# x and the first weight unit loaded, split and multiplied in halves at the start of a decoder trunk kernel

## The reference

```python
def rms_norm(x, g):
    y = xf * lax.rsqrt(jnp.mean(xf * xf, axis=-1, keepdims=True) + EPS)
    return (y * g.astype(jnp.float32)).astype(x.dtype)

def swiglu(h, w_gate, w_up, w_down):
    return (jax.nn.silu(h @ w_gate) * (h @ w_up)) @ w_down

def reference(x, meta, ...):
    h = jnp.concatenate([jnp.broadcast_to(meta...), x], axis=1)
    for l in range(DEPTH):
        f = swiglu(rms_norm(h, ffn1_pre[l]), ffn1_wg[l], ffn1_wu[l], ffn1_wd[l])
        h = h + FFN_RESID * rms_norm(f, ffn1_post[l])
        ...  # mixer (pool, short convolution, gated linear attention), then the second FFN in the same form
    return h[:, N_META:]
```

## Time and profile before

| | us |
|---|---|
| median of 3 runs (1104.22 to 1105.97) | 1104.71 |
| span of the profiled execution, first to last instruction (no other time of it is given) | 1104.4 |
| PE busy in it | 1066.6 |
| DVE, ACT, POOL busy | 659.6, 505.7, 290.9 |
| first product of x and weights (L1134) starts at | 16.20 |
| first product of the loop behind units 0 and 1 (L1102) starts at | 32.06 |

### The profile page before, as it was taken

One profiled execution on the slowest core, in us unless ns is written; L12 is line 12 of the kernel. 1 busy time (PEld: TensorE's weight loads), 2 busy tenths in 40 slices (PEclk: granted clock), 3 DMA queues, 4 the chain that ended last, 5 costly groups with the idle time before them and its releaser, 6 DMA issues.

```text
span 1104.4 us, 20089 instructions
## 1 busy us (share of the span) xinstructions
PE 1066.6 (97%) x8288; PEld 1029.7 (93%) x8288; DVE 659.6 (60%) x607; ACT 505.7 (46%) x543; POOL 290.9 (26%) x194
## 2 busy tenths in 40 slices
PE   8999999999899999999989999999998989999997
PEld 7999999988798999999979999998987989999996
DVE  5745454498776844454486444536997676555543
ACT  6444444455445543443454434435543555434441
POOL 2333330036300433340024333200372023324100
PEclk8999999999999999999999999999999999999998
DMA  9765445634324455436636553456533327563531
GB/s 297 215 197 158 143 134 182 211 129 138 115 78 153 150 166 181 155 106 196 216 101 217 176 179 120 157 174 202 156 111 116 102 91 222 166 203 113 181 106 39
DMA packets 167646, 172.55 MB, mean 156 GB/s; under 512 B 6652, under 2 KB 160536, under 8 KB 167592
## 3 DMA queue, kind: packets, MB, share of 16 engines
q1 hardware_dynamic: 167416, 171.70, 49.0%
q10 hardware_dynamic: 176, 0.07, 0.0%
HBM read 170.70 MB, written 1.05 MB: 156 GB/s over the span
## 4 chain that ended last, share of the span: by engine, by line
PE 83%; DVE 12%; ACT 2%; issue 1%; POOL 1%; DMA 1%; SPq 0%; ACTq 0%; POOLq 0%; DVEq 0%
PE ps L1102 23%; PE ps L1103 23%; PE ps L1104 23%; PE ps L1134 3%; PE ps L1119 3%; PE ps L1135 3%; DVE h L682 2%; DVE w_lo L640 2%; DVE x_lo L668 2%; PE ps L1296 2%; DVE f L674 1%; PE ps L1363 1%; ACT w_hi L424 1%; DVE r_post L985 1%; PE ps L1168 1%
## 5 line engine op out<-in xcount | busy, mean ns | idle before, releaser
L640 DVE TENSOR_TENSOR w_lo<-raw,w_hi 128x2048 fp32r<-128x2048 f32 (+2 forms) x182 | 396.0, 2180 | 321.6 <-ACT w_hi L424 321.2
L1102 PE MATMUL ps<-x_hi,w_hi 128*128 128x272 f32 (+1 forms) x1616 | 464.6, 288 | 1.6 <-DVE w_lo L640 1.6
L1103 PE MATMUL ps<-x_lo,w_hi 128*128 128x272 f32 (+1 forms) x1616 | 465.2, 288 | 0.0
L1104 PE MATMUL ps<-x_hi,w_lo 128*128 128x272 f32 (+1 forms) x1616 | 464.3, 287 | 0.0
L424 ACT ACTIVATE w_hi<-raw 128x2048 fp32r<-128x2048 f32 (+2 forms) x182 | 321.2, 1769 | 229.5 <-PE ps L1104 183.6
L1102 PEld LDWEIGHTS ps<-x_hi,w_hi 128*128 128x128 f32 x1616 | 305.9, 189 | 4.1 <-DVE w_lo L640 2.2
L1103 PEld LDWEIGHTS ps<-x_lo,w_hi 128*128 128x128 f32 x1616 | 305.4, 189 | 0.1
L1104 PEld LDWEIGHTS ps<-x_hi,w_lo 128*128 128x128 f32 x1616 | 305.2, 189 | 0.0
L1102 PE MATMUL ps<-hid_hi,w_hi 128*128 128x272 f32 (+1 forms) x528 | 152.6, 289 | 0.0
L1104 PE MATMUL ps<-hid_hi,w_lo 128*128 128x272 f32 (+1 forms) x528 | 151.3, 287 | 0.0
L1103 PE MATMUL ps<-hid_lo,w_hi 128*128 128x272 f32 (+1 forms) x528 | 150.5, 285 | 0.0
(11 more groups left out here) (163 smaller groups left out, 1047.8 us busy)
## 6 DMA issues: line engine op xcount, KB each, us to landing
raw<-in_ffn_wg SPq DMA_DIRECT2D x88, 512.0 KB, 4.0
raw<-in_ffn_wu SPq DMA_DIRECT2D x88, 512.0 KB, 4.9
raw<-in_ffn_wd SPq DMA_DIRECT2D x96, 384.0 KB, 3.2
raw<-in_w_in SPq DMA_DIRECT2D x40, 512.0 KB, 4.7
raw<-in_ffn_wd SPq DMA_DIRECT2D x32, 256.0 KB, 3.2
raw<-in_w_out SPq DMA_DIRECT2D x16, 512.0 KB, 4.5
x_tok<-in_x SPq DMA_DIRECT2D x2, 512.0 KB, 6.7
raw<-in_w_in SPq DMA_DIRECT2D x4, 256.0 KB, 3.5
```

Of the source, the lines that this page charges most:

```text
L640: v_.tensor_tensor(w_lo[:, slot, 0:n], raw[:, slot, 0:n], f32(w_hi[:, slot, 0:n]), ALU.subtract)\
L1102: pe.matmul(out_, wh, xh, start=first, stop=False)
L1103: pe.matmul(out_, wh, xl, start=False, stop=False)
L1104: return pe.matmul(out_, wl, xh, start=False, stop=last)
```

## The change

x comes in four DMAs of half the columns each (channel tiles 0 to 3, then 4 to 7), two on SP's queue and two on ACT's. Unit 0 comes in four DMAs too: k = 0 and 1 of both matrices, then k = 2 and 3. SP's order is meta, x, unit 0's first half, x, unit 0's second half, unit 1, and the parameters and constants behind it. PE transposes tiles 0 to 3, runs the `w_hi x_hi` and `w_lo x_hi` products of k = 0 and 1, transposes tiles 4 to 7, and only then does the `x_lo` products and the second half of unit 0. ACT and DVE split unit 0 in two halves, in between the tiles of x.

```diff
@@ SP
-            def first_loads():
-                sp.dma_start(meta_tok[:, :], meta).then_inc(x_in, 16)
-                for tt in range(2):
-                    sp.dma_start(x_tok[:, tt], x[0, tt * P:(tt + 1) * P, :]).then_inc(x_in, 16)
-                for name, src, per in rows[1:]:
-                    load_rows(sp, name, src, per, par_in)
+            def first_unit():
+                wg, wu, _ = weights(phases[0])
+                dst = raw[:, 0].rearrange("p (s k n) -> p s k n", s=2, k=4)
+                sp.dma_start(meta_tok[:, :], meta).then_inc(x_in[0], 16)
+                for half in range(2):
+                    cols, ks = slice(half * 512, half * 512 + 512), slice(2 * half, 2 * half + 2)
+                    landed = raw_in[0] if half else first_in
+                    sp.dma_start(x_tok[:, 0, cols], x[0, 0:P, cols]).then_inc(x_in[half], 16)
+                    sp.dma_start(dst[:, 0, ks], wg[:, ks, 0:256]).then_inc(landed, 16)
+                    sp.dma_start(dst[:, 1, ks], wu[:, ks, 0:256]).then_inc(landed, 16)
             def constant_loads():
+                for name, src, per in rows[1:]:
+                    load_rows(sp, name, src, per, par_in)
@@ ACT
+            for half in range(2):
+                cols = slice(half * 512, half * 512 + 512)
+                act.dma_start(x_tok[:, 1, cols], x[0, P:2 * P, cols]).then_inc(x_in[half], 16)
...
-            high_unit(0, UNIT)
             act.wait_ge(par_ready, 1)
-            for kk in range(KT):
+            for kk in range(2):
+                high_x(kk)
+            first_high(0)
+            for kk in range(2, 4):
+                high_x(kk)
+            first_high(1)
+            for kk in range(4, KT):
                 high_x(kk)
             high_unit(1, UNIT)
@@ DVE
-            low_unit(0, UNIT)
...
-            for kk in range(KT):
+            def copy_h(kk):
                 v_.wait_ge(ends_tr, kk + 2)
                 v_.tensor_copy(h[:, kk, :], ps[:, kk, 0:T]).then_inc(h_ready, 1)
-            for kk in range(KT - 1):
-                low_x(kk)
+            for kk in range(4):
+                copy_h(kk)
+            first_low(0)
+            low_x(0)
+            low_x(1)
+            first_low(1)
+            for kk in range(4, KT):
+                copy_h(kk)
+                low_x(kk - 2)
             low_unit(1, UNIT)
+            low_x(KT - 2)
             low_x(KT - 1)
@@ PE
+            pe.wait_ge(x_in[0], 48)
+            for kk in range(4):
+                transpose_x(kk)
+            def first_unit():
+                view = up_view(0)
+                pe.wait_ge(h_ready, 4)
+                for half in range(2):
+                    if half:
+                        pe.wait_ge(unit_lo, 1 + RING)
+                    else:
+                        pe.wait_ge(first_lo, 1)
+                    for kk in range(2 * half, 2 * half + 2):
+                        pe.wait_ge(xh_ready, kk + 1)
+                        for mm in range(4):
+                            pe.matmul(ps[:, mm, 0:T], view(w_hi, kk, mm), x_hi[:, kk, :], start=kk == 0, stop=False)
+                            pe.matmul(ps[:, mm, 0:T], view(w_lo, kk, mm), x_hi[:, kk, :], start=False, stop=False)
+                    if half == 0:
+                        pe.wait_ge(x_in[1], 32)
+                        for kk in range(4, KT):
+                            transpose_x(kk)
+                    for kk in range(2 * half, 2 * half + 2):
+                        pe.wait_ge(xl_ready, kk + 1)
+                        for mm in range(4):
+                            last = pe.matmul(ps[:, mm, 0:T], view(w_hi, kk, mm), x_lo[:, kk, :], start=False,
+                                             stop=False)
+                last.then_inc(unit_used, 1)
```

More of the change, by code:

```diff
@@ L227, in trunk @@
         mix_in = sem("mix_in")
-        x_in = sem("x_in")
+        x_in = [sem(f"x_in{i}") for i in range(2)]
+        first_in = sem("first_in")
+        first_hi = sem("first_hi")
+        first_lo = sem("first_lo")
         zeroed = sem("zeroed")
@@ L365, in _ @@
                     for j in range(2):
-                        up_unit(j, u0 + j + 1, slice(0, 256))
                         if j == 0 and u0 == 0:
-                            first_loads()
+                            first_unit()
+                        else:
+                            up_unit(j, u0 + j + 1, slice(0, 256))
                         if j == 1 and u0 == 0:
@@ L456, in high_x, with first_high @@
                 act.activation(x_hi[:, kk, :], h[:, kk, :], ACT.Copy, scale=col("ffn1_pre", 0, kk)).then_inc(xh_ready, 1)
-            high_unit(0, UNIT)
-            act.wait_ge(par_ready, 1)
-            for kk in range(KT):
+            def first_high(half):
+                tiles = lambda w: w[:, 0].rearrange("p (s k n) -> p s k n", s=2, k=4)[:, :, 2 * half:2 * half + 2]
+                if half:
+                    act.wait_ge(raw_in[0], 32)
+                else:
+                    act.wait_ge(first_in, 32)
+                act.activation(tiles(w_hi), tiles(raw), ACT.Copy).then_inc(unit_hi if half else first_hi, 1)
+            act.wait_ge(par_ready, 1)
+            for kk in range(2):
[5 more added lines that the diff above has]
+            for kk in range(4, KT):
                 high_x(kk)
@@ L713, in _, with first_low @@
             v_.sem_inc(up_evac, 1)
-            low_unit(0, UNIT)
+            def first_low(half):
+                tiles = lambda w: w[:, 0].rearrange("p (s n) -> p s n", s=2)[:, :, 512 * half:512 * half + 512]
+                if half:
+                    v_.wait_ge(unit_hi, 1)
+                else:
+                    v_.wait_ge(first_hi, 1)
+                v_.tensor_tensor(tiles(w_lo), tiles(raw), f32(tiles(w_hi)), ALU.subtract)\
+                  .then_inc(unit_lo if half else first_lo, 1)
             v_.wait_ge(ends_tr, 1)
@@ L1186, in _, with transpose_x @@
               .then_inc(ends_tr, 1)
-            pe.wait_ge(x_in, 48)
-            for kk in range(KT):
+            def transpose_x(kk):
                 if kk == KT - 1:
@@ L1195, in _ @@
                 last.then_inc(ends_tr, 1)
-            pe.wait_ge(h_ready, 4)
+            pe.wait_ge(x_in[0], 48)
[5 more added lines that the diff above has]
+                for half in range(2):
+                    if half:
+                        pe.wait_ge(unit_lo, 1 + RING)
+                    else:
+                        pe.wait_ge(first_lo, 1)
[14 more added lines that the diff above has]
+                last.then_inc(unit_used, 1)
             for ph in phases:
@@ L1208, in group @@
                             u = u0 + ja + j
+                            if u == 0 and not j and waits:
+                                first_unit()
+                                continue
                             unit(u % RING, i4 + (u + 1 + RING), up_view(u % RING), range(4 * j, 4 * j + 4), range(4),
```

2 lines of the change are left out of this document (1 added, 1 removed).

## The result

| | before | after |
|---|---|---|
| median, us | 1105.28 (4 runs, 1104.22 to 1105.97) | 1112.91 (4 runs, 1112.14 to 1113.71) |
| span of the profiled execution | 1104.4 | 1110.2 (its own time 1112.14) |
| start of unit 1's high part on ACT (H) | 17.50 | 21.29 |
| first product of the loop behind units 0 and 1 | 32.06 | 36.71 |
| from there to the end | 1072.3 | 1073.5 |

The changed kernel takes 1.0069 of the time before (95% interval 1.0055 to 1.0083): slower, as forecast, and 2.4 us above the upper end of the forecast range (1110.5). The direction was right, the time 4.4 us too low.

What follows compares the result with a forecast made beforehand. PE, busy 1066.6 of 1104.4 us, bounds the kernel, so the start counts only by delaying its long run. H later by 2.5 plus a 1.5 us slow stretch made 4.0, 1108.4; predicted 1108.5 us, range 1105.3 to 1110.5.

Steps and rivals of the forecast that it cites:

- What bounds the start: First 32 us: they count only by when PE enters its long run; POOL's adds, following ACT's squares and H, set that.
- The loads cost nothing: Start: the reordered DMAs and ACT's table load, delayed under 1 us, cost nothing, with 2 us or more of cover each.
- The chain in the new order: Start, PE, ACT and DVE: transposes, unit 0's halves, sixteen products and alternating copies make H 2.5 us later, at 20.0.
- The baseline: Whole kernel: the sum starts from the profiled span of 1104.4 us, taken as 0.3 under the median of runs shown.
- The sum: Whole kernel: 2.5 us for H plus 1.5 us for a slow stretch make 4.0 us, 1108.4 against the profiled 1104.4.
- the transposes start at about 8.2: Start of PE: transposes of x begin 2.0 us earlier, once the products of ones and the gains' transpose end.
- The stretch behind it: PE behind the wait at `sum_h`: dense products at half clock for about 3.3 us, costing 1.5 us.
- The wait at `sum_h`: PE at the end of unit 1: it waits 3.4 us for POOL's adds instead of 2.16.
- Full clock at both places: Rival, sixteen products and `sum_h`: H rises by only 1.0 and the wait stays below 3 us; 1105.7 us, chance 0.12.
- POOL ahead of unit 2's low part: Rival: POOL's fourth add starts before DVE's low part, 1.85 us come back; 1103.5 to 1105.1 us, chance 0.10.
- The early x worth its whole: Rival, start: all dates up to H move with the transposes, 2.0 us sooner; 1102.4 us, chance 0.05.
- The clock theory: Rival posed for the experiments, start of PE: the order only matters through the two half-clock stretches; no chance given.

Runs made afterwards that it cites:

- e13: The changed kernel run again, nothing altered: 1111.93 us, 1.0060 of the kernel before.
- e14: Second set of runs of the new order on PE, ACT and DVE with the old loads: 1112.42 us, 1.0062 of the kernel before.
- e2: The new loads only, with the order of the kernel before on PE, ACT and DVE: 1107.63 us, 1.0018 of the kernel before.
- e1: The kernel before with four more semaphores that nothing uses: 1105.86 us, 1.0005 of the kernel before.
- e11: Changed kernel's loads; all tiles first on PE, tiles 4 to 7 copied earlier on DVE, four squares ahead of unit 1's high part: 1104.59 us, 0.9989.
- e9: The new order on PE, ACT and DVE with the old loads, first set of runs: 1111.34 us, 1.0049 of the kernel before.
- e10: The changed kernel with unit 1's high and low parts ahead of tiles 4 to 7 on ACT and DVE: 1109.22 us, 1.0029 of the kernel before.
- e15: The changed kernel with 7 instead of 11 products of ones at the start: 1111.43 us, 1.0047 of the kernel before.
- e4: The changed kernel with five products of ones in PE's gap ahead of the sixteen products: 1109.51 us, 1.0043 of the kernel before.
- e3: The changed kernel with tiles 4 to 7 transposed on PE straight behind tiles 0 to 3, ahead of the sixteen products: 1106.90 us, 1.0013.
- e12: e11 with 7 instead of 11 products of ones at the start: 1101.30 us, 0.9974 of the kernel before.
- e16: The kernel before with 7 instead of 11 products of ones at the start: 1105.58 us, 1.0000 of the kernel before.
- e7: The kernel before with the square of each tile right behind its x_hi on ACT: 1105.57 us, 1.0002 of the kernel before.

## Why the prediction was right or wrong

**What bounds the start: right.** From the loop's first product on, the kernels measured here take 1070.8 to 1074.1 us; most of what differs between them is decided in the first 27 to 39 us.

**The loads cost nothing: right** inside the new order (e13 against e14), at least to the 0.1% that these runs can tell. As a blanket sentence it was too wide: under the old order they cost 1.7 us (e2), by a path that the forecast did not look at, the copy of the gains behind unit 0's low part. ACT's first table load came 1.03 us later (2.67 for 1.64), not under 1, and cost nothing. From the issue of the first output DMA to the program's end the kernels with new loads took 5.3 to 5.5 us, those with the old ones 5.0 to 5.1. The cause of that is open; it is small and in every one of them.

**The chain in the new order: right.** Idle ahead of the first half's low part 2.44 us (2.2 forecast), products with a pitch of 0.23, tile 4 behind them, ACT standing meanwhile, DVE's copies alternating with `x_lo` (0.76 us a tile, 0.78 forecast), H late, POOL's adds late, a wait at `sum_h`, a half-clock stretch behind it. The two `x_lo` behind unit 1's low part were priced at 0.42 us more and took 3.12 together, beside POOL's adds; DVE still waited 0.55 us for ACT behind them, so they cost nothing.

**Where it failed.** The forecast was 1108.5 and the median is 1112.91: 4.4 us, in three parts.

- *The baseline, 1.8 us.* The failed step is "its span lies 0.3 under the median of the runs shown": a span was held against times. In each execution where both are known the time is about 2.0 us over the span (after 1112.14 and 1110.2; e1 1104.79 and 1102.8), and the forecast had put 0.1 there. The profiled execution before so took about 1106.4 us. With that step right the forecast would have been 1110.4 and its range would have ended at 1112.4, still 0.5 short.
- *The sum, 1.8 us.* Forecast 1108.4 as a span, measured 1110.2. The failed term is the date "the transposes start at about 8.2", which took the 6.66 us of the products of ones in the earlier trace rows as given. They took 7.91 us, and the transposes began at 9.32. That is 1.1 of the 1.3 us by which H was late (21.29 for 20.0). The rest: 0.2 more until the sixteen products began, 3.54 us for them where 3.2 was the middle of the forecast, and 0.2 less each for tile 4 and for DVE's copies. POOL's end was 11.62 behind H, 0.3 less, because its first add took 2.19 us where it took 2.58 before (at 20.76). So `sum_h` began 3.45 us later than before, for 2.5 forecast. The stretch behind it cost 1.5, as forecast (the next norm's root on ACT is 4.97 us later: 246.27 for 241.30). From there to the first output DMA 0.5 more were lost, which no run explains, and at the program's end 0.3.
- *The draw, 0.8 us.* After's profiled run lies 0.8 us under its median.

The second part is in good part a draw as well. In e13, the same kernel, the products of ones took 6.83 us and the transposes began at 8.23, as forecast; there the clock cost more (all sixteen products at half clock, 3.90 us to tile 4, H at 20.85, and half clock behind the wait from 31.83 to 38.65). Its span was 1109.0, 0.6 over the sum, and its median 1111.93 lies above the range too. Only the baseline's error is the same in both. The same 11 products took 6.66 (before), 7.42 (e1), 7.91 (after) and 8.34 us (e11).

By the same arithmetic before's profiled run lay 1.1 us over its median. That is why the loss is 7.6 us in medians and 5.8 us between the two profiles.

**The wait at `sum_h`.** The forecast of 3.4 us was 2.99. The Trainium skill ("TensorE: Matmul & The Clock Gate", section "HAM oscillation — how this bites in real kernels") has TensorE go back to half clock behind such waits, and the traces agree for the changed kernel, e9, e10, e13 and e15. But e4 waited for 2.99 us at the same place, with 0.72 busy us of 3.60, and e14 for 2.98 us, and both kept their clock. So the length of this wait does not tell alone whether the clock falls: with 2.48 to 2.99 us it fell in five profiles (in the wait or just behind it) and not in two, with 0.74 to 2.16 us (e1, e2, e3, e11, e12, e16, before) it did not. The changed order makes the stretch likely, not certain.

**The rivals.** Full clock at both places did not occur in the changed kernel's two profiles; e4 has it, and its median is 3.4 us lower (2.4 against e13). POOL ahead of unit 2's low part did not occur: the fourth add began 0.23 us behind DVE's low part (29.09) and took 2.69 us, 0.24 and 0.22 us behind it in e13 and e15. The race was as close as forecast (0.2), but its price was wrong: in e10 POOL wins it, and the chain only moves the long add by one:

```profile
27.02 0.78 POOL pre_acc L1055
...
27.93 2.63 POOL pre_acc L1055
```

From the fourth add's start to the last one's end e10 takes 3.54 us, the changed kernel 3.59. Winning would have given nothing back. The early x worth its whole is refuted for this order and shown possible by e12. The clock theory, that the order matters through its two half-clock stretches alone, fell too: e3, with one half-clock stretch (22.4 to 25.8), is 2.6 us under e4, which has none in the start.

**What stays open.** Why PE goes over to the fast pace at another time in each execution, why the clock falls in some waits and not in others, and why the new loads end 0.4 us later.

## What to carry to other kernels

An input that lands earlier is worth only what the engines' fixed orders let through: here two of them (sixteen products ahead of tile 4 on PE, two low halves ahead of tile 4 on DVE) turned an earlier x (PE had it at 6.55 us in e12, at 10.22 before) into squares 3.8 us later. When work is split to start early, keep the short operations that others wait for (transposes, copies) together ahead of the long ones, and count what fills each idle gap, since the gap can also cost clock (here sixteen products took 3.54 us behind it, 2.1 us in e4). And compare a sum with times of one kind: a span with a span, and a profile with its own run's time, not with a median of others.

## What the runs showed of the hardware

- Transposes straight behind products ran on at full clock: in e3 PE did nothing but transposes from 8.6 to 12.9 us at 1.00, and e12 likewise. Behind a wait they did not always: in e1, with 0.75 us of wait ahead of them, the clock fell at 12.5 in the midst of them. Transposes at half clock did not bring it back: 3.00 of 3.00 us busy at 0.50 in the earlier trace rows.
- The first products of an execution ran at about half the later pace until a time that differed from run to run (4.2 us before, 6.7 after), while the granted clock was given as 1.00.
- Two executions of the same kernel differ in their clock. The changed kernel had half clock behind `sum_h` from 34.03 to 37.44 in its first profile and from 31.83 to 38.65 in e13, around waits of 2.99 and 2.97 us; from the end of the wait on PE was busy throughout.
- DVE's SCALAR_TENSOR_TENSOR beside POOL's adds: seven took 5.68 us instead of 2.97 (e7). The Trainium skill ("SBUF — State Buffer", section "Who interferes with whom") has a DVE instruction with two inputs in SBUF contend with a GpSimd instruction that reads SBUF; the trace agrees for this pair.
- Every execution took 2.0 us (1.75 to 2.18) more than its span from first to last instruction.
